# Chunked gated delta rule: another order of a step's pieces, and the output norm's sums of squares on ScalarE

## The reference

```python
def gated_delta_net(q, k, v, z, a, b, a_log, dt_bias, gdn_norm):
    ...
    kb = kh * beta[..., None]
    m = jnp.einsum('bhncd,bhnjd->bhncj', kb, kh) * decay_strict
    lhs = jnp.eye(C, dtype=f32) + m
    rhs = jnp.concatenate([vh * beta[..., None], kb * jnp.exp(gcum)[..., None]], axis=-1)
    sol = lax.linalg.triangular_solve(lhs, rhs, left_side=True, lower=True)
    value, k_cumdecay = sol[..., :Dh], sol[..., Dh:]
    attn_inner = jnp.einsum('bhncd,bhnjd->bhncj', qh, kh) * decay_incl
    ...
    def step(state, inp):
        qd, kc, val, ai, kd, gl = inp
        v_new = val - jnp.einsum('bhcd,bhde->bhce', kc, state)
        o = jnp.einsum('bhcd,bhde->bhce', qd, state) + jnp.einsum('bhcj,bhje->bhce', ai, v_new)
        state = state * jnp.exp(gl)[..., None, None] + jnp.einsum('bhcd,bhce->bhde', kd, v_new)
        return state, o
    ...
    o = o * lax.rsqrt(jnp.mean(o * o, axis=-1, keepdims=True) + EPS) * gdn_norm.astype(f32)
    o = o * jax.nn.silu(z.astype(f32).reshape(B, S, H, Dh))
```

## Time and profile before

| | us |
|---|---|
| median of 3 runs | 2871.76 |
| time of the profiled execution | 2870.19 |
| its span | 2868.5 |
| delta rule, from its first matmul to the last gate | about 1785 to 2060 of the span |
| one tile of the scan in the steady stretch | about 32 |
| TensorE, VectorE, ScalarE, GpSimd busy, over the span | 2649.3, 1699.3, 766.0, 1125.3 |

### The profile page before, as it was taken

One profiled execution on the slowest core, in us unless ns is written; L12 is line 12 of the kernel. 1 busy time (PEld: TensorE's weight loads), 2 busy tenths in 40 slices (PEclk: granted clock), 3 DMA queues, 4 the chain that ended last, 5 costly groups with the idle time before them and its releaser, 6 DMA issues.

```text
span 2868.5 us, 37231 instructions
## 1 busy us (share of the span) xinstructions
PE 2649.3 (92%) x14704; PEld 2162.1 (75%) x14704; DVE 1699.3 (59%) x2246; ACT 766.0 (27%) x1362; POOL 1125.3 (39%) x774
## 2 busy tenths in 40 slices
PE   4999888889999999999999999677699999999998
PEld 4867766777878888888876767566588888888887
DVE  6268988764766566565675783566625334444335
ACT  4235467534331001111023432232213100111002
POOL 2432465444554344354342223222263434434332
PEclk8999999999999999999999999798899999999999
DMA  6201132002311111111122110000221111111111
GB/s 219 67 12 34 37 101 69 9 31 74 117 59 48 41 58 44 44 58 42 51 74 67 44 30 22 2 2 1 96 96 52 45 44 58 44 44 58 37 51 59
DMA packets 142499, 153.49 MB, mean 54 GB/s; under 512 B 7183, under 2 KB 105252, under 8 KB 142374
## 3 DMA queue, kind: packets, MB, share of 16 engines
q1 hardware_dynamic: 137088, 143.97, 15.8%
q10 hardware_dynamic: 5286, 7.79, 0.8%
HBM read 143.35 MB, written 8.39 MB: 53 GB/s over the span
## 4 chain that ended last, share of the span: by engine, by line
PE 76%; DVE 14%; ACT 5%; issue 4%; DMA 1%; POOL 0%; ACTq 0%; SPq 0%; DVEq 0%; POOLq 0%
PE ps L1989 11%; PE ps L1991 11%; PE ps L1990 11%; PE ps L1974 11%; PE ps L1976 11%; PE ps L1975 11%; ACT sel_out L989 2%; PE ps L2383 2%; DVE yt L1796 2%; PE ps L2065 2%; DVE score L1429 1%; DVE yt L1785 1%; DVE best L1427 1%; PE ps L2143 1%; DVE u_half L1869 1%
## 5 line engine op out<-in xcount | busy, mean ns | idle before, releaser
L1974 PE MATMUL ps<-h_hi,w_hi 128*128 128x512 f32 x1472 | 585.5, 398 | 10.1 <-issue 5.6
L1975 PE MATMUL ps<-h_lo,w_hi 128*128 128x512 f32 x1472 | 575.3, 391 | 0.0
L1976 PE MATMUL ps<-h_hi,w_lo 128*128 128x512 f32 x1472 | 575.2, 391 | 0.0
L728 POOL TENSOR_TENSOR w_hi<-raw,zero 128x1024 fp32r<-128x1024 f32 x128 | 243.7, 1904 | 781.4 <-PE ps L1976 398.4
L1989 PE MATMUL ps<-w_hi,u_hi 128*128 128x512 f32 x1024 | 399.3, 390 | 0.0
L1991 PE MATMUL ps<-w_hi,u_lo 128*128 128x512 f32 x1024 | 399.1, 390 | 0.0
L1990 PE MATMUL ps<-w_lo,u_hi 128*128 128x512 f32 x1024 | 399.1, 390 | 0.0
L1118 ACT ACTIVATE act_r<-ps 128x512 f32<-128x512 f32 x128 | 76.4, 597 | 1131.9 <-PE ps L1976 1131.9
L1680 DVE TENSOR_TENSOR act_r<-act_r 128x512 f32<-128x512 f32 x128 | 165.3, 1291 | 331.1 <-ACT act_r L1118 331.1
L731 POOL TENSOR_TENSOR w_lo<-raw,w_hi 128x1024 fp32r<-128x1024 f32 x128 | 338.1, 2642 | 10.1
L1974 PEld LDWEIGHTS ps<-h_hi,w_hi 128*128 128x128 f32 x1472 | 278.0, 189 | 77.5 <-issue 17.4
(11 more groups left out here) (426 smaller groups left out, 4056.2 us busy)
## 6 DMA issues: line engine op xcount, KB each, us to landing
raw<-in_w_up_dram SPq DMA_DIRECT2D x64, 512.0 KB, 4.0
raw<-in_w_down_dram SPq DMA_DIRECT2D x64, 512.0 KB, 3.5
raw<-in_w_ada_dram SPq DMA_DIRECT2D x48, 512.0 KB, 3.7
raw<-in_w_in_dram SPq DMA_DIRECT2D x32, 512.0 KB, 3.7
raw<-in_w_out_dram SPq DMA_DIRECT2D x32, 512.0 KB, 3.5
x<-in_x_dram SPq DMA_DIRECT2D x12, 512.0 KB, 9.4
x_mid<-x SPq DMA_DIRECT2D x8, 512.0 KB, 5.5
x<-x_mid ACTq DMA_DIRECT2D x8, 512.0 KB, 7.5
```

Of the source, the lines that this page charges most:

```text
L728: g_.tensor_tensor(w_hi[:, r, :], raw[:, r, :], zero.to_broadcast([P, 1024]), ALU.add).then_inc(sem("w_hi_done"), 1)
L1974: mm(ps[:, bank, :], wh, h_hi[:, k, cols], start=(k == 0), stop=False)
L1975: mm(ps[:, bank, :], wh, h_lo[:, k, cols], start=False, stop=False)
L1976: last = mm(ps[:, bank, :], wl, h_hi[:, k, cols], start=False, stop=(k == NK - 1))
```

## The change

Three things change. The pieces of a slot come in another order: `head_z` first, `finish_a` behind the z levels, `finish_b` between levels 3 and 4 (with the level steps 4 and 5 behind it and behind the second `chunk_a`), and `tail_b` behind the k times q product of `head_b`. `head_b` is cut in two: its turn of b0, with u, is a piece of its own (`head_c`) behind `tail_b`. `finish_c` moves from slot 8 of its tile to slot 9, where the next tile's levels stand ahead of the tail. And the sums of squares of the norm are made by ScalarE, with four Square activations out of bank 7 that each add up into one column of osum, in place of one multiplication and one sum on VectorE.

```diff
-        G_ORDER = [("finish_a", 8, 0), ("chunk_a", 7, 0), ("head_a", 0, 0)]
-        G_ORDER += [("level_z", l, l) for l in range(1, 6)] + [("tail_a", 6, 0)]
-        G_ORDER += [("chunk_b", 7, 0), ("finish_b", 8, 0)]
-        G_ORDER += [("level_tu", l, l) for l in range(1, 6)]
-        G_ORDER += [("chunk_a", 7, 1), ("finish_c", 8, 0), ("tail_b", 6, 0), ("head_b", 0, 0), ("chunk_b", 7, 1), ("head_z", -1, 0)]
+        G_ORDER = [("head_z", -1, 0), ("chunk_a", 7, 0), ("head_a", 0, 0), ("finish_c", 9, 0)]
+        G_ORDER += [("level_z", l, l) for l in range(1, 6)]
+        G_ORDER += [("finish_a", 8, 0), ("tail_a", 6, 0), ("chunk_b", 7, 0)]
+        G_ORDER += [("level_tu", l, l) for l in range(1, 4)]
+        G_ORDER += [("finish_b", 8, 0), ("chunk_a", 7, 1)]
+        G_ORDER += [("level_tu", l, l) for l in range(4, 6)]
+        G_ORDER += [("head_b", 0, 0), ("tail_b", 6, 0), ("head_c", 0, 0), ("chunk_b", 7, 1)]
...
-            "dve": ["vnew0", "sdec0", "snew0", "vnew1", "sdec1", "snew1", "sq", "sum", "rec", "on", "gated"],
-            "act": ["ot", "sd"],
+            "dve": ["vnew0", "sdec0", "snew0", "vnew1", "sdec1", "snew1", "rec", "on", "gated"],
+            "act": ["ot", "sum", "sd"],
...
                     s.activation(ot, bank(7), ACT.Copy).then_inc(sem("scan_act"), 1)
+                    for h in range(GH):
+                        last = s.activation(vnew[:, h, :], bank(7)[:, h, :], ACT.Square, accum_out=osum[:, h:h + 1])
+                    last.then_inc(sem("scan_act"), 1)
                 if kind == "finish_b":
-                    act.wait_ge(sem("scan_dve"), scan_count("dve", t, "sum"))
+                    act.wait_ge(sem("scan_act"), scan_count("act", t, "sum"))
...
                     last.then_inc(prep_sem("dve", t), 1)
+                if kind == "head_c":
                     dve.wait_ge(prep_sem("mm", t), prep_count("mm", t, "turn"))
...
-                if kind == "finish_a":
-                    dve.wait_ge(sem("scan_act"), scan_count("act", t, "ot"))
-                    v.tensor_tensor(vnew, ot, ot, ALU.mult).then_inc(sem("scan_dve"), 1)
-                    dve.wait_ge(sem("scan_dve"), scan_count("dve", t, "sq"))
-                    v.tensor_reduce(osum, vnew, AX.X, ALU.add).then_inc(sem("scan_dve"), 1)
...
                     column_blocks(n0, kc[:, :, tok], qc[:, :, tok], "kq")
+                if kind == "head_c":
                     pe.wait_ge(sem("halves_ready"), 4)
```

More of the change, by code:

```diff
@@ L1886, in _ @@
                         dve.wait_ge(sem("scan_mm"), scan_count("mm", t - 1, "ai"))
-                        dve.wait_ge(sem("scan_dve"), scan_count("dve", t - 1, "sum"))
+                        dve.wait_ge(sem("scan_act"), scan_count("act", t - 1, "sum"))
                     v.tensor_tensor(vnew[r], b["val"][r], bank(6)[r], ALU.subtract).then_inc(sem("scan_dve"), 1)
```

## The result

The median of four runs is 2845.17 us (2844.08 to 2845.56), against 2871.96 before (2871.75 to 2874.03, four runs); the ratio is 0.9904, with a 95% interval of 0.9887 to 0.9922. The profiled execution took 2844.08 with a span of 2842.3, 26.1 us less than before's 2870.19, where the sum had said 31.9. The forecast was 2840, the range 2834 to 2854; the median lies 0.2 us above the upper bound of the forecast proper (2834 to 2845), at the lowest edge of rival A's.

A forecast was written before the change was run, and what follows sets the result against it. Order of work and hand-offs, with no engine full, were taken to bound the delta rule. Five steady periods 28.0 + filling 5.4 + tile 5 to 6 1.4 - tile 6 to 7 2.9 = 31.9 us saved, giving 2840 (2834 to 2854).

The forecast's parts named there:

- rival A: Steady periods: TensorE's clock still falls, 1.4 us a period reaching VectorE, 7 us for five; 2848, chance 0.22.
- The column's term: VectorE's decay column, made earlier: waits of 2.23 (product with ones) and 1.51 us (turned k) go each period.
- The new wait for level 2: VectorE after the state's update: a new wait of 1.1 us a period (0.7 to 1.5) for t and u.
- The wait for the root: VectorE before the reciprocal: waits 1.5 us a period (1.3 to 1.8) for ScalarE's root, where it was 1.78.
- Squares as a gain: Norm's square and sum leave VectorE: 1.38 us of work and a 1.03 wait for ScalarE's copy go each period.
- Filling: First tiles of the stage, decay column made early: gains of 2.7 and 2.7 us, together 5.4.
- Tile 5 to 6: No new head here: the norm's and state update's terms go, waits of 1.8, 0.1 and 1.5 come; gain 1.4 us.
- Tile 6 to 7: Level 4's subtractions come behind a state decay of 2.60 us beside GpSimd's splitting; loss 2.9 us (1.0 without splitting).
- The last tile: End of the stage: ScalarE's squares replace VectorE's square and sum; time even.
- B: ScalarE's chain to the root: squares at 1 us each, wait grows 2.6 us a tile, 18 us; 2858, chance 0.08.
- C: Delta-rule stage: a data dependence, not the order, sets the period; waits only move, 2872 within 6, chance 0.04.
- D: Half clock over the whole stage: slower, 24 us more over five periods at three quarters; 2895, chance 0.04.

The follow-up runs named there:

- The two experiments: Squares moved to ScalarE alone, against the kernel before: 2874.03 us; square and sum put back on VectorE, against the changed kernel: 2841.41 us.
- the column undone: Changed kernel with the decay column (`head_z`) last in `G_ORDER` again, all else as changed: 2864.29 us, ratio 0.9975.

## Why the prediction was right, and where it was not

- *The steady stretch: right.* 31.85 to 26.2 was forecast, 26.0 measured at full clock. The sum over five periods, 161.2 to 132.0, is 29.2 us where 28.0 was said, although two of them lost 2.0 us to the clock: a period before was 32.2 on the mean and not 31.85, and the waits that came were smaller than forecast. VectorE's busy time is 19.43, as said.
- *The terms of the period.* The column's term was right in size: the waits of 2.23 and 1.51 went and came back with it. The new wait for level 2 was 1.39 (forecast 1.1, within its 0.7 to 1.5). The terms listed for it add up to 2.2, not 1.1; they come to 1.1 without the inner attention, which in the changed kernel ends as VectorE starts the state's update. The wait for the root was 1.11 (forecast 1.5, below its 1.3). That term was mis-sized in its four squares: 0.25 us each from start to start, not 0.28 to 0.40, for in the row used the Exp itself is longer, and the read hides behind the next square. The waits of 0.1 and 0.2 for the second state products and level 3 did not show in the period above; another period has 0.15 for the first, and level 3's t is waited for 0.91 in the two periods whose clock fell.
- *Squares as a gain: only in this sum.* The sum credits the part with 1.38 + 1.03. The two experiments show that most of this credit falls into waits: the part is worth 0.4 a period in the new order and loses 0.5 to 0.9 in the old.
- *Filling: 5.4 forecast, 6.5 measured* (55.7 to 49.25 from first column to first state product). Behind the third head TensorE had its full clock earlier than before: k was turned in 0.66 us where it took 1.11, and kbe waited for nothing where it had waited 1.63.
- *Tile 5 to 6: 1.4 forecast, none measured* (24.37 and 24.38; the terms listed add up to 1.3). The waits for level 2 (2.00, said 1.8) and the root (1.11, said 1.5) were together a little better than said; then kbe waited 0.50 and level 3's t 0.88 for products at a clock of 0.60. VectorE's timeline in the changed kernel, and the stretch with the clock:

```profile
1979.47 0.85 DVE L1870 TENSOR_TENSOR t_half<-t_half,ps 64x256 f32<-64x256 f32 x2 [2.00 <-PE ps L2384]
...
1985.38 0.69 DVE L1880 TENSOR_TENSOR kbe<-ps,g_bege 128x512 f32<-128x512 f32 x1 [0.50 <-PE ps L2389]
```

```profile
1985.00:1989.00 4.00, 4.00 (x46) 3.55 (x45) 2.72 (x5) 0.36 (x1) 3.92 (x4) 0.60 0.02 4
```

- *Tile 6 to 7: 2.9 of loss forecast, 3.8 measured.* The decay of the state beside GpSimd's splitting lasted 2.07 here against 2.60 before, so the lock that the Trainium skill ("SBUF — State Buffer", "SBUF: two separate sides") describes cost 0.5 less than in the row of before. The clock of the tile fell from 0.92 to 0.80. The chain named was the right one: moving level 4 back won 1.5, and 3.6 with the clock kept up, so some 2 of the 3.8 are clock, which the forecast had not counted here.
- *The last tile: even forecast, 4.1 of loss measured.* This is the step that failed. The prediction weighed the clock only in the steady tiles and took the tail's products at before's lengths. With the clock kept, the last tile takes 14.1 us and not 14.95, so "even" was near for the work itself, and the loss is clock. The low clock from tile 6 to 7 goes with the new order: all kernels here that have it, without added products, granted 0.73 to 0.80 there, those with level 4 moved back included, and the three in the old order 0.92 to 1.00. The order alone does not decide the last tile: the same list ran it at 0.59 twice and at 0.98 once. What decides between them stays open. The last products of the tail and the first of the last tile ran at half clock (all rows here but the first), in TensorE's timeline of the changed kernel:

```profile
2003.73 0.68 PE L2384 MATMUL ps<-zp_half,t_half 64*64 64x64 f32 x16 [0.86 <-ACT zp_half L1238]
...
2006.66 1.12 PE L2389 MATMUL ps<-ident,ot 128*128 128x128 f32 x4 [2.25 <-DVE ot L1905]
...
2010.61 2.08 PE L2372 MATMUL ps<-vb,e 128*128 128x128 f32 x8 [1.13 <-DVE vb L1885]
2012.47 1.91 PE L2372 MATMUL ps<-e,kbe 128*128 128x128 f32 x8
...
2015.08 1.97 PE L2439 MATMUL ps<-state,kct 128*64 128x128 f32 x8 [0.69 <-ACT kct L1246]
```

- *Rivals.* A (the clock falls) was right in part: two of five periods, at 1.2 and 0.9 us instead of 1.4, and most of the last tile, where it had not been looked for. B had the right place and the wrong price. A clock of 0.9 or less in the steady stretch, one of the prediction's own signs of being wrong, was there in these two (0.87). C and D did not happen; TensorE's clock rose from 0.89 to 1.00 in three periods.
- Sum: 6.5 + 29.2 - 0 - 3.8 - 4.1 = 27.7 before rounding of the terms, less the 1.5 by which the stage began later, 26.2, which is the difference of the spans. Against the 31.9 of the sum, the filling and the periods gave 2.3 more than said and the three last tiles 6.5 less. That these errors point opposite ways, and that the steady clock fell in only two periods, is in part luck.

## What to carry to other kernels

When no engine is full and each works through one list, write a period as the busy time of the engine whose turn comes in every step plus its waits, and look for the independent operation that stands last ahead of a wait: moving it was worth far more here than taking work off that engine. Work moved to another engine is priced by the wait that it lands in, which here made the same edit a small loss in one order and a small gain in the other. Cost the first and last tiles by their own rows, clock included, since a reordering made for the full stretch can uncover there what it hid.

## What the runs showed of the hardware

An activation with an accumulator on 128 x 128 out of PSUM, with its read, cost 0.25 us from start to start, though the two rows last 0.27 and 0.20: each overlaps the next. With eight products of no use (0.94 us each at full clock) in the last two tiles, the last one went from 19.0 us to 14.1. The same work can meet either clock: over the 16.25 us ahead of the last tile TensorE was busy for 9.85 us in the changed kernel and 9.86 with the column undone, with the same instructions, and the last tile then ran at 0.59 and at 0.98. The first state product of that tile (8 matmuls) took 1.97 us in the one and 1.09 in the other.
